# A hybrid decoder layer on one core: another order of the weight blocks in the gated recurrence

## What is computed

```python
xa = causal_conv(lru_x, conv_w[i], conv_b[i])                  # 4 taps, per channel
gate_a = sigmoid(blockwise(xa, w_a) + b_a)                     # 16 blocks of 80 channels
gate_x = sigmoid(blockwise(xa, w_x) + b_x)
log_a = -LRU_C * gate_a * softplus(-lam)
a = exp(log_a)
u = xa * gate_x * sqrt(1.0 - exp(2.0 * log_a))
h = scan(a, u)                                                 # h[t] = a[t] * h[t-1] + u[t]
o_a = (h * gelu(lru_y)) @ w_lru_o[i]
```

## Time and profile before

| | before |
|---|---|
| median of 3 runs | 2814.91 us (2812.26 to 2815.58) |
| the profiled execution | 2812.64 us |
| its span, first to last instruction | 2810.8 us |
| TensorE, share of the span with a matmul in flight | 98% |
| VectorE | 58% |
| ScalarE | 34% |
| GpSimd | 34% |
| first turn of the gated recurrence | about 1206 to 1349.5 us |
| second turn | about 1349.5 to 1493 us |

### The profile page before, as it was taken

One profiled execution on the slowest core, in us unless ns is written; L12 is line 12 of the kernel. 1 busy time (PEld: TensorE's weight loads), 2 busy tenths in 40 slices (PEclk: granted clock), 3 DMA queues, 4 the chain that ended last, 5 costly groups with the idle time before them and its releaser, 6 DMA issues.

```text
span 2810.8 us, 60971 instructions
## 1 busy us (share of the span) xinstructions
PE 2741.2 (98%) x25491; PEld 2287.8 (81%) x25491; DVE 1631.8 (58%) x1807; ACT 956.0 (34%) x1447; POOL 942.9 (34%) x691
## 2 busy tenths in 40 slices
PE   5999999999999999999999999999999999999999
PEld 4798989898989898988787777788888788888887
DVE  4645454545454545469694666466648643333896
ACT  5312121212121212135555768301113333334343
POOL 0403030303030303034343111233333477777443
PEclk9999999999999999999999999999999999999999
DMA  5202020202020202033332111366511133234353
GB/s 211 74 22 61 21 61 21 61 21 61 21 61 21 61 21 61 11 116 115 119 112 72 34 62 50 118 196 211 173 58 45 53 113 113 85 100 142 124 170 92
DMA packets 255359, 235.00 MB, mean 84 GB/s; under 512 B 24353, under 2 KB 213883, under 8 KB 255099
## 3 DMA queue, kind: packets, MB, share of 16 engines
q1 hardware_dynamic: 241632, 183.74, 21.7%
q10 hardware_dynamic: 13467, 47.31, 4.8%
HBM read 184.08 MB, written 46.92 MB: 82 GB/s over the span
## 4 chain that ended last, share of the span: by engine, by line
PE 92%; DVE 3%; ACT 2%; issue 1%; DMA 0%; SPq 0%; POOL 0%; ACTq 0%; DVEq 0%; POOLq 0%
PE ps L306 68%; PE ps L1243 3%; PE ps L1257 3%; PE ps L1254 2%; PE ps L1221 2%; PE ps L1306 1%; PE ps L1443 1%; PE ps L1468 1%; PE ps L1211 1%; PE ps L1456 1%; PE ps L1177 1%; PE ps L1263 1%; PE ps L1290 1%; PE ps L1280 1%; PE ps L1309 1%
## 5 line engine op out<-in xcount | busy, mean ns | idle before, releaser
L306 PE MATMUL ps<-x_hi,w_hi 128*128 128x512 f32 (+1 forms) x2372 | 801.4, 397 | 6.1 <-issue 2.0
L306 PE MATMUL ps<-x_hi,w_lo 128*128 128x512 f32 (+1 forms) x2372 | 783.2, 390 | 0.0
L306 PE MATMUL ps<-x_lo,w_hi 128*128 128x512 f32 (+1 forms) x2372 | 782.9, 390 | 0.0
L296 POOL CAST w_hi<-w_raw 128x1024 fp32r<-128x1024 f32 (+2 forms) x161 | 153.5, 954 | 1544.8 <-PE ps L306 1292.2
L306 PEld LDWEIGHTS ps<-x_hi,w_hi 128*128 128x128 f32 (+1 forms) x2372 | 436.8, 187 | 114.5 <-issue 22.4
L306 PEld LDWEIGHTS ps<-x_hi,w_lo 128*128 128x128 f32 (+1 forms) x2372 | 443.9, 187 | 96.8
L306 PEld LDWEIGHTS ps<-x_lo,w_hi 128*128 128x128 f32 (+1 forms) x2372 | 444.2, 187 | 92.6
L298 POOL TENSOR_TENSOR w_lo<-w_raw,w_hi 128x1024 fp32r<-128x1024 f32 (+2 forms) x161 | 329.3, 2045 | 12.9
L306 PE MATMUL ps<-x_sums,w_hi 128*128 128x512 f32 x648 | 201.7, 392 | 0.6 <-issue 0.6
L1054 POOL TENSOR_TENSOR w_lo<-arena,w_hi 128x384 fp32r<-128x384 f32 (+1 forms) x124 | 154.6, 1248 | 111.2 <-ACT w_hi L2216 111.2
L2519 DVE COPY_PREDICATED arena<-hid,ps 128x256 f32<-128x256 int32 x144 | 72.0, 500 | 139.4 <-PE ps L1254 88.6
(11 more groups left out here) (346 smaller groups left out, 4449.2 us busy)
## 6 DMA issues: line engine op xcount, KB each, us to landing
w_raw<-in_w_in SPq DMA_DIRECT2D x78, 512.0 KB, 3.9
arena<-in_w_ada SPq DMA_DIRECT2D x48, 512.0 KB, 5.8
arena<-gates_sig ACTq DMA_DIRECT2D x40, 512.0 KB, 4.3
w_raw<-in_w_ffn_in SPq DMA_DIRECT2D x26, 512.0 KB, 4.0
gates_sig<-arena ACTq DMA_DIRECT2D x24, 512.0 KB, 2.7
under<-in_w_ffn_in SPq DMA_DIRECT2D x18, 512.0 KB, 5.7
hidden_sums<-arena SPq DMA_DIRECT2D x36, 256.0 KB, 2.6
under<-hidden_sums SPq DMA_DIRECT2D x11, 768.0 KB, 5.8
```

The costliest lines, as they stand in the source:

```text
L296: nc.gpsimd.tensor_copy(hi, raw).then_inc(s_whi, 1)
L306: ins = nc.tensor.matmul(dst[h], wp, xp[h], start=first and m == 0, stop=last and m == 2, skip_group_check=on)
```

## The change

The list gets another order. Each of x2, x3 and x4 moves one place ahead, y0, y1 and y2 (and with them their gate products) one back. Nothing else is edited.

```diff
-LRU_ORDER = [("x", 0), ("x", 1), ("y", 0), ("x", 2), ("y", 1), ("x", 3), ("y", 2), ("x", 4), ("y", 3), ("y", 4)]
+LRU_ORDER = [("x", 0), ("x", 1), ("x", 2), ("y", 0), ("x", 3), ("y", 1), ("x", 4), ("y", 2), ("y", 3), ("y", 4)]
```

## The result

The new order takes 2859.61 us (median of 4 runs, 2858.37 to 2863.4) against 2814.78 us: +44.8 us, a ratio of 1.0165 with a 95% interval of 1.0153 to 1.0177. Forecast were 2857 us and +43.

The account below looks back on a forecast made before the run. The gated recurrence was taken as TensorE-bound, so new waits set the cost: 10.7 + 7.0 + 1.5 + 2.3 = 21.5 us per turn, +43 us over two turns, 2857 us; range 2838 to 2877 us.

Parts of the forecast that it names:

- Step 1: Ahead of gate product 3: TensorE waits for VectorE's low(3, 2), with one block covering the chain; 10.7 us per turn.
- Step 2: Ahead of y2: its weight load queues behind the later_ada(1) wait and four ada loads; TensorE waits 7.0 us per turn.
- Step 3: At x4 and y4: small waits for GELU copies that free the PSUM pairs; 1.5 us more per turn.
- Step 4: Behind the two long waits: matmuls slowed by a halved TensorE clock; 2.3 us per turn, bounds 0 to 5.
- That only gate product 3 would wait: Rival: y2's weights come in time, only gate product 3 waits; +26 us, 2840 us, chance 0.14.
- That only y2 would wait: Rival: VectorE, idle through y2's wait, brings low(3, 2) in 10.9 us; +17 us, 2831 us, chance 0.04.
- or nothing: Rival: no effect, as the waits fall on time that TensorE loses anyway; chance 0.03.
- That one wait would feed the next: Rival: low(2, 2) or y4's weights come late too; from +62 us on, 2877 us or more, chance 0.07.
- An order with a gain: Rival: earlier x blocks take the halo chain off gate products 1 and 2; 2.7 us won at most, 2811 us, chance 0.02.

Follow-up runs that it names:

- conv_early: The new order with VectorE's convolutions 2 to 4 moved up to where the x blocks now arrive, ada loads unmoved; 2849.27 us against 2814.54 before the change.
- ada_behind_y: The new order with the ada loads moved back behind the y blocks (positions 3, 5, 7, 8); 2845.47 us against 2814.54 before the change.
- both: The new order with ada loads back behind the y blocks and VectorE's convolutions moved up; 2827.26 us against 2814.54 before the change.

## Why the prediction was right, step by step

**What bounds the kernel.** Right, though the 2.7 us of the earlier trace rows are not quite all: by PE's timeline TensorE waited 1.47 us in turn 1 and 1.40 in turn 2, with 0.25 us for GpSimd's L298 and 1.11 us of issue at the stage's end. With next to no wait of TensorE to remove, the question was what the order makes it wait for, and all the experiments move the time by the waits of TensorE and the slow stretches behind them.

**Step 1, gate product 3.** Forecast 10.7 us (9.0 to 13), measured 11.07 and 10.94. The chain is the one that was followed: gate product 2 ends at 1324.85, conv(4) at 1337.74 + 6.67 = 1344.41, low(3, 2) at 1346.81, which is 22.0 us where 20.33 were read from before and 21.6 taken. The extra is in conv(4), whose three steps took 6.67 us and not 4.85. The split of y4's weights ran beside them, from 1337.69 to 1342.01, as assumed; that it is what made them longer was not tested by itself. conv_early takes conv(4) off this chain, and 7.5 us of the wait go.

**Step 2, y2's weights.** Forecast 7.0 us (6.0 to 10.9), measured 8.44 and 8.57. By its terms, from the end of gate product 0 at 1257.33 (G): low(1, 2) ended at G + 21.3 (21.4 forecast), later_ada(1) took 7.38 us and ended at G + 32.7 (6.1 and 31.5), the load was issued 2.9 us later (2.5) and landed in 7.7 (7.2), the split took 4.3 (4.4). later_ada(1) was mis-sized by 1.3 us: its first step took 3.42 us beside GpSimd's subtraction and the other three 1.29 each. The Trainium skill's rule, page "SBUF — State Buffer", section "SBUF: two separate sides", is an exclusive lock held for the whole instruction. The trace agrees: GpSimd's subtraction ran from 1281.71 to 1284.96, the step that started at 1282.63 ended 1.1 us after it, and 7.38 lies within the 5.1 to 8.4 us that the rule gave. The halo copy that was to slip behind x3's copy did (ScalarE, 1275.23 and 1276.28):

```profile
1275.23 1.03 ACT L1942 ACTIVATE arena<-ps 128x1024 f32<-128x1024 f32 x1 [7.66 <-issue]
1276.28 1.06 ACT L1949 ACTIVATE hid<-arena 64x1024 fp32r<-64x1024 f32 x1
```

and gate product 1 started without a wait, at G + 21.9.

**Step 3, small waits.** Forecast 1.5 us more per turn; measured about 0. x4 waited 0.71 us for the GELU copy (1.1 forecast). y4 did not wait for it: the copy ended at 1353.04, and gate product 3, which was to take 5.44 us, took 8.15, from 1346.96 to 1355.11 (7.39 in turn 2). And the waits at the turn's end fell from 1.47 us (0.27, 0.95 and 0.25) to 0.82. The error is that steps 3 and 4 were added where one covers the other.

**Step 4, the clock.** Forecast 2.3 us per turn (0 to 5), measured 4.3 and 5.0: a turn grew by 23.84 and 24.58 us, the waits by 19.57 in either. The rows of the half-clock stretches give the same by another way: 2.91 + 5.44 us of work there in turn 1 and 5.98 + 3.91 in turn 2, half of which is 4.2 and 4.9. This is the term that was too small, at the upper end of its bounds: 1.5 and 3.0 us behind y2's wait, where 1.5 were taken, and 2.7 and 2.0 behind gate product 3's, where 0.8 were. Whether the slow start of the kernel, from which the bound came, was the lower level, the trace doesn't show: its granted clock reads 1.00 there. The rule of the Trainium skill, page "TensorE: Matmul & The Clock Gate", section "What's actually happening", that idleness throttles the clock, is borne out by the windows above: granted 0.50 after each long wait, 1.00 at the same place when the wait is filled.

**The sum.** 21.5 us per turn were forecast, 23.8 and 24.6 measured in the profiled execution; step 1 (+0.3), step 2 (+1.5) and step 4 (+2 to 3) were too small, step 3 (-1.5) too large. The profiled execution is the slowest of the four (2863.4 us) and has two short half-clock stretches outside the stage; by medians the change costs 44.8 us against 43. The mechanism was right at each of the two long waits; that the total came as near as 44.8 to 43 is partly luck: the error of step 3 took back part of those of steps 2 and 4, and the one execution whose rows are known lost 48.4 us in the stage alone.

**Rivals.** That only gate product 3 would wait did not happen, but ada_behind_y is just that kernel: 2845 us where the rival gave 2840, with 2.1 us of slow matmuls per turn where it had 0.8. That only y2 would wait, or nothing, falls with the waits of 11.07 and 10.94 us at gate product 3. That one wait would feed the next is what the main rival of the experiments tested; it does not, each wait goes by its own edit. An order with a gain was excluded because conv(2) and conv(4) stand behind gated_input; with them moved up the kernel is still slower than before.

## What to carry to other kernels

An order of blocks is shared by every queue that follows it, and by none that is written out by hand: when blocks are exchanged, count for each consumer how much work stands ahead of it afterwards, against the chain that feeds it. A list position may also carry something else (here ada loads and the wait for their tiles); whatever load stands behind it in the same queue inherits both the wait and the bytes ahead. And where TensorE is busy throughout, a wait may cost more than its length: here 19.6 us of waits cost 24 us per turn, because matmuls behind them ran at half the clock, while a neighbouring small wait vanished under that.

## What was not expected of the hardware

- The granted clock fell to half also where no wait of TensorE over 1 us stood before it. The new kernel's own profile has two such places outside the stage, the first right behind a wait of 0.87 us, the second behind one of 0.45 us and 16 one-column matmuls (length, busy of PE, PEld, DVE, ACT, POOL, clock, DMA share, GB/s):

```profile
912.00:915.60 3.60, 3.60 (x58) 3.48 (x59) 0.94 (x4) 0.00 (x0) 0.00 (x0) 0.53 0.00 0
2195.60:2199.00 3.40, 3.40 (x10) 2.62 (x9) 2.92 (x10) 0.00 (x0) 0.00 (x0) 0.50 0.00 0
```

The same code in the kernel before, with waits of 0.58 and 0.45 us, kept a clock of 1.00, and other runs had such stretches at other places (1050.8 and 2173.8 us in ada_behind_y). What brings them was not found. The clock also fell after a wait was over: in the kernel both, gate product 3 started after 3.54 us of waiting at a granted clock of 1.00, and 0.50 was granted from about 0.8 us later in turn 1 and 1.3 in turn 2.

- Taking the waits away from TensorE with useless matmuls removed the slow stretches behind them and won nothing in total: +47.6 us against before with them, +44.8 without.
